# Moving the first weight sums of the paired pieces to GpSimd, and pairing one more piece, in a two-layer decoder trunk

## What is computed

```python
def _conv_ffn(x, w_up, conv_w, conv_b, w_down):
    h = x @ w_up
    ...
    return (jax.nn.silu(gate) * up) @ w_down          # (256, 5632) @ (5632, 2048)

for i in range(DEPTH):                                # DEPTH = 2
    ...
    f = _conv_ffn(x, ffn_w_up[i], ffn_conv_w[i], ffn_conv_b[i], ffn_w_down[i])
    x = _layernorm(DEEPNORM_ALPHA * x + f, ln2_g[i], ln2_b[i])
```

## Time and profile before

| | |
|---|---|
| median of 3 runs | 2085.57 us (2085.12 to 2086.72) |
| profiled execution, its time | 2084.49 us |
| profiled execution, its span | 2082.7 us |
| PE busy | 2077.0 us of the span |
| DVE / ACT / POOL busy | 1529.5 / 1215.3 / 2.7 us |
| granted TensorE clock | 1.000 |

### The profile page before, as it was taken

How to read it: one execution, slowest core, us unless ns; L and a number is a source line. 1 busy time by engine, 2 the same in 40 slices (tenths; PEclk the granted TensorE clock), 3 DMA queues, 4 the chain that set the end, 5 groups by cost and what they waited for, 6 DMA issues and landing times.

```text
span 2082.7 us, 38940 instructions
## 1 busy us (share of the span) xinstructions
PE 2077.0 (100%) x14554; PEld 1916.0 (92%) x14554; DVE 1529.5 (73%) x2716; ACT 1215.3 (58%) x2222; POOL 2.7 (0%) x12
## 2 busy tenths in 40 slices
PE   9999999999999999999999999999999999999999
PEld 8999889999999998888888888899999999988887
DVE  6767777767766669888766558667766677688888
ACT  5645566556555555655656666566555565555654
POOL 0000000000000000000000000000000000000000
PEclk9999999999999999999999999999999999999999
DMA  9655666565655556556554454745655656565554
GB/s 348 235 176 167 210 219 213 188 201 181 201 190 192 196 176 212 183 201 223 192 168 165 167 177 167 256 153 193 201 192 191 198 185 198 169 218 181 204 202 162
DMA packets 201631, 408.97 MB, mean 196 GB/s; under 512 B 7616, under 2 KB 9152, under 8 KB 200768
## 3 DMA queue, kind: packets, MB, share of 16 engines
q1 hardware_dynamic: 201392, 407.45, 57.5%
q10 hardware_dynamic: 144, 0.26, 0.0%
HBM read 404.53 MB, written 3.15 MB: 196 GB/s over the span
## 4 chain that ended last, share of the span: by engine, by line
PE 98%; DVE 1%; DMA 0%; SPq 0%; ACT 0%; issue 0%
PE acc L1846 32%; PE acc L1848 32%; PE acc L1847 32%; PE acc L2177 0%; DMA head_first<-in_first 0%; PE acc L2151 0%; PE acc L1959 0%; PE acc L2201 0%; PE acc L1952 0%; PE acc L2209 0%; DVE x_tok L1817 0%; PE acc L2047 0%; SPq L563 0%; DVE x_tok L1822 0%; PE acc L2261 0%; PE acc L2282 0%
## 5 line engine op out<-in xcount | busy, mean ns | idle before, releaser
L1105 DVE TENSOR_TENSOR w_lo<-raw,w_hi 128x512 fp32r<-128x512 f32 x1330 | 878.5, 686 | 398.3 <-ACT w_hi L662 394.5
L662 ACT ACTIVATE w_hi<-raw 128x512 fp32r<-128x512 f32 x1330 | 804.6, 629 | 559.3 <-PE acc L1848 549.1
L1846 PE MATMUL acc<-ffn_xT,w_hi 128*128 128x256 f32 x2920 | 806.7, 276 | 0.0
L1847 PE MATMUL acc<-ffn_xT,w_hi 128*128 128x256 f32 x2920 | 806.2, 276 | 0.0
L1848 PE MATMUL acc<-ffn_xT,w_lo 128*128 128x256 f32 x2920 | 806.2, 276 | 0.0
L1847 PEld LDWEIGHTS acc<-ffn_xT,w_hi 128*128 128x128 f32 x2920 | 548.4, 188 | 0.1
L1846 PEld LDWEIGHTS acc<-ffn_xT,w_hi 128*128 128x128 f32 x2920 | 548.2, 188 | 0.1
L1848 PEld LDWEIGHTS acc<-ffn_xT,w_lo 128*128 128x128 f32 x2920 | 548.1, 188 | 0.0
L1846 PE MATMUL acc<-w_hi,ffn_act 128*128 128x512 f32 (+1 forms) x642 | 234.6, 365 | 0.0
L1847 PE MATMUL acc<-w_lo,ffn_act 128*128 128x512 f32 (+1 forms) x642 | 234.6, 365 | 0.0
L1848 PE MATMUL acc<-w_hi,ffn_act 128*128 128x512 f32 (+1 forms) x642 | 234.5, 365 | 0.0
(11 more groups left out here) (318 smaller groups left out, 1949.4 us busy)
## 6 DMA issues: line engine op xcount, KB each, us to landing
raw<-in_ffn_w_up SPq DMA_DIRECT2D x172, 1024.0 KB, 5.0
raw<-in_ffn_w_down SPq DMA_DIRECT2D x88, 1024.0 KB, 5.1
raw<-in_diff_w_in SPq DMA_DIRECT2D x38, 1024.0 KB, 5.4
raw<-in_w_out SPq DMA_DIRECT2D x32, 1024.0 KB, 5.1
raw<-in_pool_w_in SPq DMA_DIRECT2D x16, 1024.0 KB, 5.1
raw<-in_mem_w_kv SPq DMA_DIRECT2D x12, 1024.0 KB, 12.3
next_from_raw<-in_ffn_w_up SPq DMA_DIRECT2D x4, 1024.0 KB, 10.2
head_first<-in_first SPq DMA_DIRECT2D x5, 768.0 KB, 11.0
```

The costliest lines, as they stand in the source:

```text
L662: nc.scalar.activation(hi, raw_place(st, c, k, j), ACT.Copy).then_inc(hi_made, 1)
L1105: nc.vector.tensor_tensor(lo, raw_place(st, c, k, j), hi.bitcast(F32), ALU.subtract).then_inc(lo_made, 1)
L1846: pe.matmul(out, w[0], x[0], start=start, stop=False, skip_group_check=True)
L1847: pe.matmul(out, w[0], x[1], start=False, stop=False, skip_group_check=True)
```

## The change

POOL gets a loop at the end of its program (`sum_right_block`). For each paired piece of both layers, in order, it waits until the lo parts of everything up to the piece before the previous one are made and until the piece is loaded. Then it makes sums 0 and 1, with two instructions of 128x512 instead of DVE's one of 128x1024. DVE keeps steps 1 and 2. Step 1 stands behind granule 3 of the piece ahead, step 2 behind unit 0 of the paired piece itself. Piece 7 of chunk 3 in layer 0 becomes a paired piece, so there are 24. With it, `pair_outputs` of that chunk moves from behind piece 7 to behind piece 9, and ACT's copy with it. `pair_outputs` no longer uses `conv` for its first result but a part of `gb`, and it waits once more for its own semaphore.

```diff
-DOWN_PAIRS = (((), PAIRED, PAIRED, PAIRED[:3]), ((), PAIRED, PAIRED, PAIRED))
+DOWN_PAIRS = (((), PAIRED, PAIRED, PAIRED), ((), PAIRED, PAIRED, PAIRED))
...
+        def sum_right_block(st, c, k):
+
+            pool.wait_ge(lo_made, st.granule(c, k - 1, 0))
+            pool.wait_ge(piece_loaded[k % SLOTS], st.loaded(c, k))
+            right = blocks(k, 1, 2).rearrange("p q a n -> p q (a n)")
+            for place, block in ((0, 0), (1, 3)):
+                ins = nc.gpsimd.tensor_tensor(by_pair(sum_place(place)), right, blocks(k, block, block + 1).rearrange("p q a n -> p q (a n)"), ALU.add)
+            ins.then_inc(strassen_summed, 1)
+
+        for st in s_down:
+            for c, k in st.order:
+                sum_right_block(st, c, k)
...
             nc.vector.tensor_tensor(lo, unit_source(k, UNITS[i]), hi.bitcast(F32), ALU.subtract).then_inc(lo_made, 1)
+            if i == 0:
+                sum_weights(st, c, k, 2)
...
-                if k + 1 < st.pieces and is_paired(st, c, k + 1) and j < 3:
-                    sum_weights(st, c, k + 1, j)
+                if k + 1 < st.pieces and is_paired(st, c, k + 1) and j == 3:
+                    sum_weights(st, c, k + 1, 1)
...
-            v, w = conv[:, 0, 0, 0:HALF], gb[:, 1, 0:HALF]
+            v, w = gb[:, 0, HALF:CHUNK], gb[:, 1, 0:HALF]
             dve.wait_ge(strassen_copied, COPIED * l + PAIR_PARTS + c)
             order.done(nc.vector.tensor_tensor(v, gb[:, 0, 0:HALF], acc[:, left, HALF:CHUNK], ALU.add))
-            order.then(nc.vector.tensor_tensor(w, v, acc[:, right, HALF:CHUNK], ALU.add))
-            order.done(nc.vector.tensor_tensor(gb[:, 0, HALF:CHUNK], acc[:, right, 0:HALF], v, ALU.subtract))
+            order.done(nc.vector.tensor_tensor(w, v, acc[:, right, HALF:CHUNK], ALU.add))
+            order.done(nc.vector.tensor_tensor(v, acc[:, right, 0:HALF], v, ALU.subtract))
```

More of the change, by code:

```diff
@@ L1111, in lo_unit @@
             nc.vector.tensor_tensor(lo, unit_source(k, UNITS[i]), hi.bitcast(F32), ALU.subtract).then_inc(lo_made, 1)
+            if i == 0:
+                sum_weights(st, c, k, 2)
         def sum_weights(st, c, k, step):
[L1115 to L1126, removed]
+            dve.wait_ge(strassen_summed, st.sum_count(c, k, step))
+            before, block = ((0, 3), (2, 2))[step - 1]
+            nc.vector.tensor_tensor(by_pair(sum_place(step + 1)), by_pair(sum_place(before)),
+                                    blocks(k, block, block + 1).rearrange("p q a n -> p q (a n)"), ALU.add).then_inc(strassen_summed, 1)
         def lo_piece(st, c, k):
```

## The result

The changed kernel takes 2089.14 us (median of 13 runs, 2087.77 to 2092.52), the kernel before 2084.90 us (13 runs beside them, 2084.16 to 2086.72). The ratio is 1.0021, with a 95% interval of 1.0014 to 1.0029: slower by 4.2 us. The prediction was 2088.4 us, between 2086.0 and 2091.0, and no change that can be told. The forecast rested on a median of 2085.57 for the kernel before, so what it gave as a difference was 2.85 us, and what has to be explained is 4.2. By the prediction's own limit (slower from 2089.74 us) the median still counts as no change that can be told. The 13 runs tell more: the interval lies wholly above 1, so the kernel is slower by a little.

A forecast was written before the change was run, and what follows sets the result against it. PE was taken as the bound, busy 2077.0 of 2082.7 us. +2.74 us at the end of layer 0 and +0.11 at piece 10 of layer 1 gave +2.85 on a median of 2085.57: 2088.4 us, range 2086.0 to 2091.0.

The forecast's parts named there:

- Part 1: Chunk 3, layer 0: pairing one more piece takes 0.63 us off PE, a gain only if nobody makes PE wait behind it.
- Part 2: Down projections: DVE loses a 1.22 us instruction for each of 23 pairs, some 28 us; costed at nothing for the time.
- Part 3: End of layer 0: later `pair_outputs` starts DVE's norm 2.85 us later; PE passes the norm 2.74 us later, 0.63 gain included.
- Part 4: Piece 10 of layer 1: the additional wait in `pair_outputs` makes PE's wait there 0.11 us longer.
- Part 5: DVE's new wait for POOL's sums, read at pieces 3 to 5 of layer 0: 1.2 us per instruction, costing nothing.
- 48 instructions near 1.2 us: Expected sign in the profile after, if the forecast is right: POOL's new instructions and their length.
- rival A: At every pair, DVE and POOL block each other and PE waits: some 4 to 9 us, 2092 to 2097; chance 12%.
- its own sign of being wrong as a whole: Whole prediction wrong if PE's busy time falls by more than 0.6 us or the pairs' granules come late.
- C: End of layer 0: PE's new idle time lowers its clock, 2.2 us more at half clock, 2090.6; chance 3%.
- the forecast's own range: Whole kernel: 2.4 + 0.1 to 3.1 + 0.1 above the median, with the runs' spread 2087.4 to 2090.

The follow-up runs named there:

- experiment 5: The changed kernel, but POOL fills sums 0 and 1 with zeros instead of adding, so it reads nothing; 2088.58 us, ratio 1.0017.
- experiment 2: The kernel before with only piece 7 of chunk 3, layer 0, paired and DVE making all sums; 2087.74 us, ratio 1.0014.
- experiment 3: The kernel before, piece 7 plain, with only `pair_outputs` of chunk 3, layer 0, and ACT's copy moved behind piece 9; 2088.52 us, ratio 1.0018.
- experiment 7: The changed kernel with the five `pair_outputs` instructions of chunk 3, layer 0, cut to 16 columns each; 2086.09 us, ratio 1.0007.
- experiment 4: The changed kernel with sum steps 1 and 2 back behind granules 1 and 2 of the piece ahead; 2088.85 us, ratio 1.0020.
- experiment 9: The changed kernel with extra PE transposes at the end of layer 0, 15 ahead of the first normed transposes, 6 ahead of the second; 2088.53 us, ratio 1.0017.
- experiment 10: The changed kernel with the 15 extra PE transposes ahead of the first normed transposes alone; 2088.80 us, ratio 1.0017.

## Why the prediction was right, and where it was not

**Part 1** held. In the changed kernel PE begins piece 8 at 988.60 - 0.42 = 988.18, the very number of the prediction. The gain of 0.63 us is real and is spent behind it.

**Part 2** held in what it cost, nothing, and was wrong in what it said DVE gains. The instruction of 1.22 us left, but over the whole program DVE stands still for POOL about as long (the 26 us of experiment 5, and 7.3 us of idle time ahead of step 1). There was no relief to be carried anywhere.

**Part 3** held by its own steps: `pair_outputs` starts 2.00 us behind piece 8, ends 2.96 us later (2.95 was put), the residual step comes at 1000.36, and the additional wait makes two instructions start 0.45 us apart. PE went on 2.77 us later, and over the whole norm the loss was 2.65 us, 2.74 predicted. Experiments 2 and 3 show it without POOL, and experiment 7 that it follows the length of `pair_outputs` one for one.

**Part 4** held: 0.125 us against 0.11.

**Part 5** is the first step that failed. POOL's instruction takes 1.20 to 1.28 us where nothing holds it up, near the 1.2 put, but 1.63 us on average, so "48 instructions near 1.2 us" did not hold. "So POOL by itself costs nothing" was worked out at pieces 3 to 5 of layer 0 alone, where DVE has idle time in front of the granules. In chunk 1 of layer 1 it has none, and the start of POOL that the prediction put at its semaphore comes only when DVE lets it through (1915.02 instead of 1912.70). In the kernel before DVE worked there for some 29 us without a gap, between these two rows of it in time:

```profile
1896.92 0.69 DVE L1105 TENSOR_TENSOR w_lo<-raw,w_hi 128x512 fp32r<-128x512 f32 x1 [5.63 <-ACT w_hi L662]
...
1927.64 0.69 DVE L1105 TENSOR_TENSOR w_lo<-raw,w_hi 128x512 fp32r<-128x512 f32 x1 [1.18 <-ACT w_hi L662]
```

So there was no room for POOL's 2.40 us, which became a wait of DVE, and the two steps moved behind the granules gave up the 0.5 to 0.7 us pauses between granules in which they used to hide. Price: 0.74 us, 0.29 for the moved steps and 0.45 for the rest. It is rival A's mechanism at one place in the program, not at every pair: the other pairs have the slack that the prediction read. The prediction also named its own sign of being wrong as a whole, pairs' granules that come late. By that sign it failed in this chunk; the time stayed in the range because the chunk's price is small.

**The rival that was mis-sized is C.** Its mechanism was right, and its price was near: 2.2 us were put, and the changed kernel's executions below 1.000 lie 2.06 us above the others (1.2 to 2.6 in experiments 2 to 5), while the two profiled falls cost 1.5 and 2.6 us. Its chance was not: 3% was given to something that happens in about half the executions of the kernels with this idle stretch (3 of 11 to 8 of 13). It isn't one case or the other. It is a share of the executions, so it belonged in the sum: it moved the median by 0.7 us (the remainder of the first section) to 0.9 us (experiment 9) or 1.15 us (the changed kernel's median against that of its five executions at 1.000).

The sum thus reads 2.65 + 0.125 + 0.74 + 0.7 = 4.2 us instead of 2.85; the last term is the remainder and was not measured by itself. So the forecast of the difference is 1.4 us short, and that the predicted time is only 0.7 us off is largely luck: the median of the kernel before was taken as 2085.57 from three runs, and is 2084.9. There is a slip in the forecast's own range too: its lower end is 2085.57 + 2.5 - 0.45 = 2087.6, not 2087.4, which changes nothing here.

## What to carry to other kernels

A piece of work that stands in front of an engine's last wait is free up to the length of that wait; the same work behind it moves everything that follows one for one, whatever was taken off that engine earlier. When work goes to a second engine, look for the place where the first one has no gap at all, not for the typical place, and compare its busy time afterwards: time in which an issued instruction stands still counts as busy. And an idle stretch of PE like the 1.5 to 1.8 us here can have a second price, the clock, which one profile may not show: look at the granted clock of every execution.

## What was not expected of the hardware

- PE's clock fell to 1.2 GHz behind an idle stretch of 1.52 us (experiment 3) and of 1.74 us (experiment 5), each followed by four transposes, and stayed there for 3.4 and 6.8 us. The mean clock was below 1.000 in 27 of 56 executions with such a stretch. Where the only idle stretch was of 0.8 us (experiments 7 and 10) it was below in none of 22.
- Of POOL and DVE, neither goes first by right. DVE's four granules in a row (2.49 us) kept POOL out until their end, for 2.3 us, and DVE then waited 2.42 us for POOL's sums; where POOL had started first, the granules took 4.42 or 3.71 us.
